# A hybrid decoder step: the sample group's value products on column halves instead of column quarters

## The reference

```python
def _sel_attend(q, q_pos, ks, vs, key_pos, valid, rel_bias):
    ...
    logits = jnp.einsum('btgrd,btgksd->btgrks', q, ks).astype(jnp.float32) * SM_SCALE + bias.astype(jnp.float32)
    mask = ((dist >= 0) & valid[..., None])[:, :, :, None]
    p = _masked_softmax(logits.reshape(bsz, t, g, r, k_top * s), mask.reshape(bsz, t, g, 1, k_top * s))
    return jnp.einsum('btgrks,btgksd->btgrd', p.reshape(bsz, t, g, r, k_top, s).astype(vs.dtype), vs)
...
def _window_dense(q, q_pos, k, v, k_pos, rel_bias):
    ...
    p = _masked_softmax(logits, ((dist >= 0) & (dist < WINDOW))[:, None, None, :])
    return jnp.einsum('btgrl,blgd->btgrd', p.astype(v.dtype), v)
...
    o = g[:, :, 0] * o_c + g[:, :, 1] * o_s + g[:, :, 2] * o_w
```

## Time and profile before

| | |
|---|---|
| median of 3 timed runs | 914.32 us (912.7 to 914.93) |
| the profiled execution: time, and its span | 913.02 us, 910.9 us |
| granted TensorE clock, mean over the span | 0.994 |
| PE busy with matmuls | 863.3 us |
| DVE, ACT, POOL busy | 620.5, 368.6, 122.6 us |
| sample group, rounds 1 to 4 | about 697 to 795 us from the start |

### The profile page before, as it was taken

How to read it: one execution, slowest core, us unless ns; L and a number is a source line. 1 busy time by engine, 2 the same in 40 slices (tenths; PEclk the granted TensorE clock), 3 DMA queues, 4 the chain that set the end, 5 groups by cost and what they waited for, 6 DMA issues and landing times.

```text
span 910.9 us, 15526 instructions
## 1 busy us (share of the span) xinstructions
PE 863.3 (95%) x5973; PEld 551.3 (61%) x5973; DVE 620.5 (68%) x1149; ACT 368.6 (40%) x878; POOL 122.6 (13%) x129
## 2 busy tenths in 40 slices
PE   6999999999999999999899998998887989999997
PEld 4666665666666666767675766765654666544442
DVE  4598788999988988998557557566775567321222
ACT  4311234311021211025777887876765656411111
POOL 0011120000001011110103131232243220000000
PEclk9999999999999999999999999999999999999999
DMA  8443651431135066540750010000029987522211
GB/s 310 173 139 119 225 197 60 54 62 55 61 121 190 27 215 219 201 138 24 273 220 1 15 79 2 2 1 1 2 93 399 359 319 292 188 103 70 81 64 41
DMA packets 32109, 118.31 MB, mean 130 GB/s; under 512 B 3433, under 2 KB 11771, under 8 KB 22971
## 3 DMA queue, kind: packets, MB, share of 16 engines
q0 software_dynamic: 9360, 68.16, 20.3%
q1 hardware_dynamic: 19053, 43.39, 13.8%
q10 hardware_dynamic: 3623, 5.76, 3.0%
HBM read 108.33 MB, written 13.29 MB: 134 GB/s over the span
## 4 chain that ended last, share of the span: by engine, by line
PE 78%; DVE 11%; DVEq 3%; ACT 3%; issue 2%; DMA 1%; another core or an unknown queue 0%; ACTq 0%; POOL 0%; POOLq 0%
PE PS L836 28%; PE PS L2181 12%; PE PS L1616 6%; PE PS L1626 6%; PE PS L1644 5%; PE PS L812 3%; PE PS L2000 3%; DVE main L609 3%; PE PS L2061 2%; ACT main L1417 2%; PE PS L2025 2%; PE PS L2038 2%; DVE main L606 2%; PE PS L1599 1%; PE PS L801 1%
## 5 line engine op out<-in xcount | busy, mean ns | idle before, releaser
L836 PE MATMUL PS<-main 128*128 128x352 f32 (+1 forms) x1056 | 328.0, 469 | 0.0
L836 PEld LDWEIGHTS PS<-main 128*128 128x128 f32 x1056 | 200.4, 191 | 119.6 <-issue 1.5
L1417 ACT ACTIVATE main<-PS,main 128x512 f32<-128x512 f32 (+3 forms) x192 | 104.0, 562 | 48.7 <-DVE main L1457 24.5
L2181 PE MATMUL PS<-main 128*128 128x512 f32 x256 | 111.6, 593 | 0.0
L437 ACT ACTIVATE main<-PS 128x384 f32<-128x384 f32 x24 | 11.8, 490 | 201.7 <-PE PS L836 195.5
L1626 PE MATMUL PS<-cst,main 128*128 128x128 f32 x528 | 73.7, 282 | 15.0 <-ACT main L1417 12.5
L647 DVE SCALAR_TENSOR_TENSOR main<-main,par 128x1022 f32<-128x1022 f32 (+16 forms) x66 | 83.8, 1270 | 5.3 <-issue 0.4
L606 DVE TENSOR_TENSOR main<-main 128x1024 f32<-128x1024 f32 x64 | 75.4, 1220 | 11.6 <-DMA main<-in_cmp_k_dram,row 7.9
L2181 PEld LDWEIGHTS PS<-main 128*128 128x128 f32 x256 | 47.9, 190 | 58.1 <-issue 58.0
L609 DVE TENSOR_TENSOR main<-main 128x1024 f32<-128x1024 f32 (+2 forms) x96 | 75.0, 781 | 7.2
L1626 PEld LDWEIGHTS PS<-cst,main 128*128 128x128 f32 x528 | 57.7, 142 | 30.2 <-ACT main L1417 22.8
(11 more groups left out here) (320 smaller groups left out, 1032.1 us busy)
## 6 DMA issues: line engine op xcount, KB each, us to landing
main<-in_w_tiles_dram SPq DMA_DIRECT2D x24, 512.0 KB, 3.6
out_dram<-main SPq DMA_DIRECT2D x18, 256.0 KB, 2.1
main<-in_x_prompt_dram SPq DMA_DIRECT2D x8, 512.0 KB, 8.4
main<-in_w_out_dram SPq DMA_DIRECT2D x4, 1024.0 KB, 7.8
main<-in_x_prompt_dram SPq DMA_DIRECT2D x16, 256.0 KB, 3.0
out_dram<-main SPq DMA_DIRECT2D x4, 512.0 KB
diag<-in_win_k_dram SPq DMA_DIRECT2D x8, 256.0 KB
diag<-in_win_v_dram SPq DMA_DIRECT2D x8, 256.0 KB
```

Source lines behind the costliest of these rows:

```text
L836: last = pe.matmul(bank(3 * s + j)[:, 0:w], ring[:, s, k * P:(k + 1) * P], xT[:, k, t0:t0 + w], start=(k == 0), stop=(k == KD - 1))
L1417: last = act.activation(prob[:, k % 2, g, h * nk_ * P:(h + 1) * nk_ * P], score_set(k, g)[:, h * nk_ * P:(h + 1) * nk_ * P], ACT.Exp, scal ...
L2181: last = pe.matmul(out_bank(m, h), proj[:, MIX[k], n * P:(n + 1) * P], wo[:, k, h * 512:(h + 1) * 512], start=(x == 0), stop=(x == KD - 1))
```

## The change

The value products, the blocks and the new tokens' values work on column halves. For each 128 tokens there are two matmuls, one for each sample: 64 columns of probabilities are stationary (both kv groups' query rows), and all 128 channels of the value row move. Half of what is computed (a group's rows with the other group's channels) is left unused. The result takes 128 columns of PSUM each for pages, window and blocks, and the new tokens' scores lie where the blocks come later. `finish` works on 128 columns, and adds the blocks directly.

Apart from that, in round 0, ACT copies three quarters of an odd chunk: the first sample's other 64 partitions too, by one more instruction for each of the four odd chunks; DVE copies only the second sample's, 512 columns instead of 1024.

```diff
         def gather(p):
             o = bank(6 + p % 2)
-            return o[:, 0:HD], o[:, HD:2 * HD], o[:, 2 * HD:3 * HD], o[:, 3 * HD:3 * HD + P], o[:, 3 * HD + P:3 * HD + P + 2 * DS]
+            return o[:, 0:P], o[:, P:2 * P], o[:, 2 * P:3 * P], o[:, 3 * P:4 * P], o[:, 2 * P:2 * P + 2 * DS]
+
+        def sample_rows(b2):
+            return slice(b2 * Q, (b2 + 1) * Q)
...
                     if swapped(c):
+                        if r == 0 and b2 == 0:
+
+                            act.activation(o[HD:2 * HD], i[0:HD], ACT.Copy)
                         o, i = o[0:HD], i[HD:2 * HD]
                     act.activation(o, i, ACT.Copy).then_inc(SEM["kt_act"], 1)
...
-                dve.tensor_scalar(osb1, window, sm[:, 45:46], None, ALU.mult)
+                dve.tensor_scalar(osb, window, sm[:, 45:46], None, ALU.mult)
                 dve.drain()
-                dve.scalar_tensor_tensor(osb1, pages, sm[:, 44:45], osb1, ALU.mult, ALU.add)
+                dve.scalar_tensor_tensor(osb, pages, sm[:, 44:45], osb, ALU.mult, ALU.add)
                 dve.drain()
-
-                dve.tensor_tensor(osb.rearrange("p (k d) -> p k d", k=2), osb1.rearrange("p (o d) -> p o d", o=1).to_broadcast([P, 2, HD]),
-                                  blocks.rearrange("p (o d) -> p o d", o=1).to_broadcast([P, 2, HD]), ALU.add).then_inc(SEM["o_sb"], 1)
+                dve.tensor_tensor(osb, osb, blocks, ALU.add).then_inc(SEM["o_sb"], 1)
...
-                dve.tensor_copy(ktc[HD:2 * HD, k % 4].rearrange("p b n -> p (b n)"), keys_bank(r, c, 0, 2)[0:HD]).then_inc(SEM["kt_dve"], 1)
+                first = 1 if r == 0 else 0
+                dve.tensor_copy(ktc[HD:2 * HD, k % 4, first:].rearrange("p b n -> p (b n)"),
+                                keys_bank(r, c, first, 2 - first)[0:HD]).then_inc(SEM["kt_dve"], 1)
...
-                        for b2, g, q in QUARTERS:
+                        for b2 in range(2):
                             at_ = (4 * c + j) * P % 2048
                             v = values_half(p, c // (NC // 2))[:, b2, at_:at_ + P] if c < NC else vw_d[:, b2, j * P:(j + 1) * P]
-                            last = pe.matmul(gather(p)[0 if c < NC else 1][q:q + 32, :], ptd2[:, c % 2, j * P + q:j * P + q + 32], v[:, g * HD:(g + 1) * HD],
+                            last = pe.matmul(gather(p)[0 if c < NC else 1][sample_rows(b2), :], ptd2[:, c % 2, j * P + b2 * Q:j * P + (b2 + 1) * Q], v,
                                              start=(c in (0, NC) and j == 0), stop=False)
```

More of the change, by code:

```diff
@@ L976, in program @@
         mask2 = kcn_flat[:, 640:768]
-        osb, osb1 = kcn_flat[:, 768:896], kcn_flat[:, 896:960]
+        osb = kcn_flat[:, 768:896]
         gd = sb("gd", [P, 4, 3])
@@ L2048, in blocks @@
                     pe.wait_ge(SEM["dpair"], p - 1)
-                for b2, g, q in QUARTERS:
-                    pe.matmul(gather(p)[2][q:q + 32, :], ptd[:, p * P + q:p * P + q + 32], vcn[:, 2 * p + b2, g * HD:(g + 1) * HD], start=True, stop=True)
+                for b2 in range(2):
+                    pe.matmul(gather(p)[2][sample_rows(b2), :], ptd[:, p * P + b2 * Q:p * P + (b2 + 1) * Q], vcn[:, 2 * p + b2, :], start=True, stop=True)
             def values(p, c):
@@ L2068, in new_values @@
                 pe.wait_ge(dp_sb[c % 2], p_par(p, c) + 1)
-                for b2, g, q in QUARTERS:
-                    last = pe.matmul(gather(p)[k][q:q + 32, :], ptd2[0:2 * DS, c % 2, k * P + q:k * P + q + 32],
-                                     vn[0:2 * DS, (2 * p + b2) * P + g * HD:(2 * p + b2) * P + (g + 1) * HD], start=False, stop=True)
+                for b2 in range(2):
+                    last = pe.matmul(gather(p)[k][sample_rows(b2), :], ptd2[0:2 * DS, c % 2, k * P + b2 * Q:k * P + (b2 + 1) * Q],
+                                     vn[0:2 * DS, (2 * p + b2) * P:(2 * p + b2 + 1) * P], start=False, stop=True)
                 if k == 1:
```

## The result

| | kernel before | changed kernel |
|---|---|---|
| median of 20 runs each | 914.45 us (910.86 to 918.31) | 917.59 us (916.77 to 919.35) |
| profiled execution: time, span | 913.02, 910.9 us | 917.9, 915.8 us |

The ratio is 1.0041 (95% interval 1.0032 to 1.005): the changed kernel is slower by 3.7 us, with 3.1 us between the medians. Forecast were +5.7 us and 920.0 us, in a range of 914 to 927. The runs of the changed kernel also lie in a band of 2.6 us, those of before in one of 7.5 us.

What follows compares the result with a forecast made beforehand. PE's stream and its interruptions were taken to bound rounds 1 to 4. Streaming +16.9, stalls given back -10.5 and round 0 -0.7 us made +5.7 us, 920.0 us against the median of 914.32, range 914 to 927.

Steps and rivals of the forecast that it cites:

- What bounds the kernel: Rounds 1 to 4: PE's stream and its interruptions set the end; DVE and ACT have slack. PE busy 95% of span.
- The price of the pair: Value matmuls, rounds 1 to 4: full slot 1.90 us instead of 1.03, streaming +16.9 us in all.
- The relief: Rounds 1 to 3: halving value instructions removes nearly all PE stalls, -10.5 us, bounds 0 and -12.5.
- all nine groups: Disturbed value groups on PE in rounds 1 to 3: 21.3 us instead of 9.6 free, put down to missing instructions.
- The 43 packets: Instruction queue q8 in the profile after: about 43 packets instead of 48, a sign to check.
- Round 0: Key copies: shorter DVE copies save time, ACT's added copy is hidden; -0.7 us, bounds +2 and -2.1.
- The sum: Whole execution: +16.9 - 10.5 - 0.7 = +5.7 us, 920.0 us against the median of 914.32.
- That stalls stay: Rounds 1 to 3: PE's stalls remain, +16.2 us, 930.5 us; chance 0.12, wholly or by half.
- halves don't overlap: Value matmuls: a set's two matmuls run one after the other, 957 us; chance 0.02.
- a set goes by its records: Value matmuls: 16 ns a record, so sets take half as long, 893 us; chance 0.03.
- the second rival: PE stalls, rounds 1 to 3: DMA traffic itself (port or memory) holds PE up, 930.5 us; chance 0.12, wholly or by half.
- Not slower: Rounds 0 to 3: starvation costs more than the disturbed groups show, relief 16.9 us, 914.3 us; chance 0.18.

Runs made afterwards that it cites:

- third: Kernel before with two value matmuls instead of four per 128 tokens, 64 stationary columns, only 64 channels moving (old streaming, output wrong): ratio 0.9922, 906.32 us.
- fourth: Changed kernel with the old four value matmuls of 32 stationary columns per 128 tokens, all 128 channels moving (new streaming): ratio to before 1.0098, 922.80 us.
- seventh: Kernel before with later gathers of keys and values cut to an eighth of their bytes, output wrong: ratio 0.9869, 899.92 us.
- halves in slots 2 and 4: Kernel before's quarters, but column halves in second and fourth slots of rounds 1 to 3 and each pair's first 128 tokens; round 0 copies changed: ratio 0.9999, 913.83 us.
- halves in slots 1 and 3: Changed kernel with column halves only in the first and third slots of rounds 1 to 3, quarters elsewhere: ratio to before 0.9930, 904.90 us.
- before again: Kernel before, unedited, timed and profiled once more: ratio 0.9998, 913.56 us.
- copies only: Kernel before with only the changed key copies of round 0, values on quarters as before: ratio 0.9999, 913.04 us.
- halves in slot 1: Changed kernel with column halves only in the first slot of rounds 1 to 3, quarters elsewhere: ratio to before 0.9937, 908.65 us.
- halves in rounds 1 to 3: Changed kernel with quarters again in round 4, each into its own 64 of 128 result columns: ratio to before 1.0019, 912.74 us.
- tiny matmuls: Changed kernel with 32 added 64 x 8 matmuls on constants in each full slot of rounds 1 to 4: ratio to before 1.119, 1019.99 us.
- halves only: Changed kernel with the key copies of round 0 taken back to those of the kernel before: ratio to before 1.0054, 918.61 us.

## Why the prediction was right

**What bounds the kernel: right.** Rounds 1 to 4 follow PE; DVE and ACT never held it up in them after the change.

**The price of the pair: right.** The prompt's matmuls gave 1.90 us a slot, and it is 1.90. The window chunk grew by 0.43 us (794.03 to 794.62 before, 798.33 to 799.35 now), a single set by 0.12 to 0.14 (the blocks of round 4 took from 779.55 to 779.68, now from 780.15 to 780.42). Round 4 was forecast at +4.2 and came at +4.26 us, where nothing else moves.

**The relief: right in kind, its size 1.5 us too small.** 10.5 us were taken, and rounds 1 to 3 gave back about 12.0, near the 12.5 set as the bound. The third, fourth and seventh runs show the condition: many instructions, and the gathers' bytes. The Trainium skill, Runtime: NRT & Kernel Launch, section Instruction fetch mechanics, calls the cost of crossing a block of 256 instructions mostly hidden. In rounds 1 to 3 of the kernel before it isn't: 3.3 of the 7.05 us of idle time end at every 256th PE instruction (last section). In the changed kernel, with a third fewer matmul records in rounds 1 to 4 (1234 instead of 1863; 10% fewer over the whole launch), it is.

**The reason as I put it was too coarse, and in part is not shown.** I took all nine groups for a lack of instructions. The traces have two kinds of gaps, nearly half and half. For those at block ends it is shown that instructions come late. For those inside a block, among them, it is not: PE goes on three times, at 712.33, 713.10 and 713.84 us, while the instruction queue brings nothing. The queues of that stretch of the kernel before, 711.37 to 714.41 us, are the gathers' alone:

```profile
q0 software_dynamic: 160, 1.18, 95.6%
```

What is shown for them is that fewer instructions at the same streaming, or fewer gathered bytes, take them away. That the gathers' traffic holds up what a dense stream of small matmuls reads, its weight loads for example, explains them as well; no run here parts the two. The 43 packets, a sign that the forecast named, speak for neither, as they follow from the instruction count alone (256 to a packet). That the relief came in full is to this extent luck: halves thin out the stream for either cause.

I also compared a round's average of 43 records per us with a supply of 42, as if an average decided. The run with halves in slots 2 and 4 has nearly the average of the one with slots 1 and 3 and keeps its stalls. The gaps inside a block go with a dense group right behind a gather of keys: they begin 1.0 to 1.6 us after its issue in the kernel before. For the change as made, both readings give the same forecast, since it relieves every group. For a next step they part: slots 2 and 4 against slots 1 and 3 is 0.9999 against 0.9930, 6.3 us.

**Round 0: a little more than half.** 0.4 us against 0.7 (0.6 in the second set). The first side step did come earlier by the 0.5 us forecast (3.61 us after the start of L1595 instead of 4.14), but the next wait for DVE, at 681.5 us, grew from 0.57 to 0.99. A clock effect comes on top (below).

**The sum.** +4.9 us in the profiled execution against +5.7. The medians differ by only 3.1, the ratio gives 3.7. The profiled executions of before (913.02 and 912.66) lie under their medians; in which of its stages an ordinary execution of before loses another 1 to 2 us was not seen. The rule on overhead that the forecast weighed (the Trainium skill, TensorEngine Tiling (Array Packing), section Instruction Overhead) played no part: round 4 halves its value instructions too and shows the full growth, 4.26 us.

**The rivals.** That stalls stay, that halves don't overlap, and that a set goes by its records are all excluded by the slot of 1.90 us without gaps. Of the second rival, that DMA traffic holds PE up, only the form in which the count doesn't matter is excluded. "Not slower" needed 14.2 us of relief, and 12.0 came.

## What to carry to other kernels

An idle stretch in the middle of a group of matmuls, put down to "issue", was removed here by fewer and longer instructions, even at twice the streamed columns; it pays only in the groups where the stretches are. Before a change of form over the whole loop, list the stalls by place, and set them beside the times at which large loads are issued and beside the packets of the instruction queue: the same form in 6 of 16 slots gave -0.7%, in all of them +0.4%. And where a form exists elsewhere in the kernel, its row gives the price within a few hundredths of a us.

## What the runs showed of the hardware that was not expected

**Nearly half of the idle time stands at every 256th instruction of PE, behind an instruction packet.** Count all of PE's entries in the trace of the kernel before, matmuls, weight loads and those of its sequencer, in the order of their starts: there are 12,294, or 256 to each of the 48 packets of q8. Three of the gaps end at the entries 9410, 10178 and 10946 (to within one), which lie 768 apart. The second of them:

```profile
756.34 0.85 PE L2061 MATMUL PS<-main 128*32 128x64 f32 x46
758.69 0.52 PE L2061 MATMUL PS<-main 128*32 128x64 f32 x18 [1.50 <-issue]
```

A packet of q8 ended at 757.20 us, 1.5 us before PE went on. The same entries in four traces with the same PE instructions, each as idle time in front / time since the end of the last packet, in us:

| entry | before | before again | copies only | gathers cut down |
|---|---|---|---|---|
| 9410 | 0.75 / 1.4 | 0.96 / 1.3 | 0.41 / 1.2 | 0 / 4.6 |
| 10178 | 1.50 / 1.5 | 1.50 / 1.4 | 0.40 / 1.3 | 0 / 3.7 |
| 10946 | 0.80 / 1.3 | 0.52 / 1.3 | 0.80 / 1.4 | 0.88 / 1.4 |

In the kernel before, every 256th entry from 8386 to 10946 comes 1.3 to 1.7 us after a packet's end, with a gap or without; in rounds 1 to 3 of the changed kernel the distance is 4.6 to 9.0 us. So PE waits there for its instructions; with the gathers cut down the packets come earlier at the first two of these entries, not at the third. With a fourth gap of this kind, of 0.28 us, these are 3.3 us of the 7.05. Copies only has two more, 0.76 us near entry 8386 and 1.18 near 10434.

**The rest stands inside the blocks, and its cause is open.** 3.7 us in the kernel before, all in the first and third slots of rounds 1 and 2, where a gather of keys has just been issued; round 3 gathers no keys and has none. (Two other runs, halves in slots 2 and 4 and in slot 1, have one of 0.4 us in round 3's window chunk, after a gather of values.) They repeat within a few records from trace to trace: in the four traces whose values are all in four instructions for 128 tokens and whose gathers are whole, after 24 or 25 records in the first slot of round 1 and after 30 to 33 in its third. In three of the four groups no packet of q8 moves between the start of the gap and PE's going on.

**The late start of round 0 does not come with the kernel.** In the four traces of the second set (halves in rounds 1 to 3, halves in slots 1 and 3, the tiny matmuls, gathers cut down) it is absent, and round 0, measured as for the copies above, takes 20.8 to 21.4 us; in the ten other traces it is 24.1 to 25.3 us. The tiny matmuls and the mixed forms change nothing of the key copies, scores and gathers up to there. It is about 4 us, as much as the whole effect studied. All four traces without it are of one set, so it may go with the chip or the moment. What holds DVE and ACT there was not found.

**After it, the granted clock can fall.** PE stood idle for 2.85 us in round 0 of the changed kernel, and the next scores took 1.90 us instead of 1.02. The stage of the changed kernel and that of the kernel before, PEclk third from the end:

```profile
688.00:692.00 4.00, 2.13 (x17) 0.47 (x18) 1.33 (x6) 0.85 (x2) 1.87 (x2) 0.67 0.99 377
```

```profile
688.00:692.00 4.00, 2.34 (x24) 1.02 (x24) 0.81 (x5) 1.20 (x2) 2.05 (x3) 1.00 1.00 395
```

A part of the stretch is at the lower level of 1.2 GHz, after an idle stretch of 2.85 us; the kernel before, idle for 2.04 us at the same place, keeps 2.4 GHz. Of the first set's runs three had the fall in these 4 us (halves only 0.63, copies only 0.67, old instructions with new streaming 0.76) and one had none (half the instructions); of the third set's, halves in slot 1 had it (0.77, and 0.50 in the next 4 us), and the changed kernel profiled again did not (1.00). So it does not belong to the kernel. Nor does the length of that idle stretch alone decide: halves only fell after 1.99 us, while the changed kernel, the second time, kept 2.4 GHz after 2.31 us.
